# Layer 1's attention of a two-layer decoder trunk: the heads' first keys move from its prologue into the first step's filler

## What is computed

```python
h = x @ w_in_b[j]                                   # layer 1: 768 + 768 + 768 + 256 columns
q, k, v, q_mem = jnp.split(h, [qb, 2 * qb, 2 * qb + vb], axis=-1)
o = diff_attention(q, k, v, lam, slopes_b)          # softmax of two halves of a head, a = p0 - lam * p1
mix = rms_norm(o, subln_g[j]) * (1.0 - lam_init)
mem_out = memory_attention(q_mem, mem, w_mem_kv[i])
y = jnp.concatenate([mix, mem_out], axis=-1) @ w_out[i]
x = layer_norm(DN_ALPHA * x + y, ln_g[i, 0], ln_b[i, 0])
f = moe_ffn(x, ...)                                 # 64 experts, top 8 of 4 groups, one shared expert
x = layer_norm(DN_ALPHA * x + f, ln_g[i, 1], ln_b[i, 1])
```

## Time and profile before

| | |
|---|---|
| median of three runs | 1210.28 us (1208.69 to 1210.51) |
| profiled execution, its time | 1209.24 us |
| its span | 1207.3 us, granted clock 0.997 |
| TensorE busy | 1158.9 us (96%) |
| VectorE, ScalarE, GpSimd busy | 346.2, 299.5, 64.0 us |
| moved by DMA | 446.92 MB, 370 GB/s in the mean |

### The profile page before, as it was taken

The page is one execution under the profiler, slowest core; times in us unless marked ns, Lnnn a source line. Parts: engine busy times, 40 slices in busy tenths (PEclk is TensorE's granted clock), DMA queues, the critical chain, the costliest instruction groups (busy, mean ns, idle before and its releaser), DMA issues.

```text
span 1207.3 us, 22685 instructions
## 1 busy us (share of the span) xinstructions
PE 1158.9 (96%) x8946; PEld 708.4 (59%) x8948; DVE 346.2 (29%) x904; ACT 299.5 (25%) x713; POOL 64.0 (5%) x102
## 2 busy tenths in 40 slices
PE   9999999999999999998999999999999899999985
PEld 6875755555555555555687648555555555555552
DVE  1435612222122212221514456221222222222214
ACT  1453312222121212221213433122221212122212
POOL 1341000000001000000012100000000010000000
PEclk9999999999999999999999999999999999999998
DMA  9943799999999999999990558999999999999995
GB/s 359 365 176 128 308 414 416 421 422 422 422 422 420 410 420 421 422 421 420 389 361 24 203 233 335 410 419 421 422 422 422 422 415 403 404 421 422 422 421 209
DMA packets 74502, 446.92 MB, mean 370 GB/s; under 512 B 6976, under 2 KB 12480, under 8 KB 24896
## 3 DMA queue, kind: packets, MB, share of 16 engines
q1 hardware_dynamic: 72208, 441.22, 89.4%
q10 hardware_dynamic: 2224, 4.72, 1.0%
HBM read 444.86 MB, written 1.05 MB: 369 GB/s over the span
## 4 chain that ended last, share of the span: by engine, by line
PE 74%; DMA 17%; issue 4%; DVE 2%; POOL 1%; SPq 0%; ACT 0%; DVEq 0%; POOLq 0%
DMA ring<-in_w_up 16%; PE bank L1235 16%; PE bank L1216 14%; PE bank L1269 14%; PE bank L772 7%; PE bank L791 6%; PE bank L1277 4%; PE bank L830 4%; PE bank L1242 1%; PE bank L1092 1%; PE bank L806 1%; PE bank L1115 1%; PE bank L993 1%; POOL soft L731 1%; PE bank L761 1%
## 5 line engine op out<-in xcount | busy, mean ns | idle before, releaser
L1235 PE MATMUL bank<-ring,work 128*64 128x256 f32 x1952 | 225.4, 380 | 13.2 <-DMA ring<-in_w_up 13.0
L1216 PE MATMUL bank<-ring,work 128*64 128x256 f32 x1984 | 227.8, 382 | 8.9 <-DMA ring<-in_w_gate 8.7
L1269 PE MATMUL bank<-ring,work 128*32 128x512 f32 x1904 | 222.0, 595 | 0.3
L1216 PEld LDWEIGHTS bank<-ring,work 128*64 128x64 f32 x1984 | 141.3, 137 | 116.9 <-issue 58.1
L1235 PEld LDWEIGHTS bank<-ring,work 128*64 128x64 f32 x1952 | 147.5, 137 | 81.5 <-issue 20.4
L1938 DVE SCALAR_TENSOR_TENSOR yhalf<-bank,gcol,yhalf 128x512 fp32r<-128x512 f32 x124 | 93.1, 751 | 214.7 <-ACT yhalf L1562 214.7
L1930 DVE TENSOR_TENSOR work<-work,bank 128x256 f32<-128x256 f32 x64 | 26.9, 421 | 366.7 <-PE bank L1235 366.7
L1562 ACT ACTIVATE yhalf<-bank,gcol 128x512 fp32r<-128x512 f32 x124 | 85.2, 687 | 181.4 <-PE bank L1269 181.4
L1269 PEld LDWEIGHTS bank<-ring,work 128*32 128x32 f32 x1904 | 57.4, 109 | 116.9 <-issue 110.0
L1399 ACT ACTIVATE work<-bank 128x512 f32<-128x512 f32 (+4 forms) x177 | 77.9, 440 | 98.0 <-PE bank L772 46.3
L1399 ACT ACTIVATE back<-bank 128x128 fp32r<-128x128 bf16 x64 | 17.7, 277 | 280.5 <-PE bank L1188 280.5
(11 more groups left out here) (190 smaller groups left out, 819.1 us busy)
## 6 DMA issues: line engine op xcount, KB each, us to landing
ring<-in_w_gate SPq DMA_DIRECT2D x124, 1024.0 KB, 13.7
ring<-in_w_up SPq DMA_DIRECT2D x122, 1024.0 KB, 15.7
ring<-in_w_down SPq DMA_DIRECT2D x119, 1024.0 KB, 14.9
ring<-in_w_in_b SPq DMA_DIRECT2D x3, 3072.0 KB, 18.6
ring<-in_w_out SPq DMA_DIRECT2D x4, 2048.0 KB, 14.6
home<-in_w_gate SPq DMA_DIRECT2D x4, 1024.0 KB, 17.9
ring<-in_w_down SPq DMA_DIRECT2D x8, 512.0 KB, 13.3
ring<-in_w_in_a ACTq DMA_DIRECT2D x1, 3072.0 KB, 19.5
```

Of the source, the lines that this page charges most:

```text
L1216: last = pe.matmul(gate_bank[slots_of(e), 0:HID], xg[:, k, slots_of(2 * j + e)], w[e][:, k, :], start=(k == 0), stop=(k == KT - 1))
L1235: last = pe.matmul(up_bank[slots_of(e), 0:HID], xg[:, k, slots_of(2 * j + e)], w[e][:, k, :], start=(k == 0), stop=(k == KT - 1))
L1269: last = pe.matmul(yb[half][rows_of(t, e), :], hT[b][:, f, slots_of(e, t)], w[e][:, f, half * 512:half * 512 + 512], start=(f == 0), stop= ...
```

## The change

It takes k0 (and the wait for its weight item in1) out of the prologue of layer 1 and puts it into filler 0. q0 moves from filler 0 to filler 1, k1 from 1 to 2, where it stands before va; vb moves from filler 2 to 3, before q1. The table of groups gets k0 behind qm. The copies out of the banks move with their groups: VectorE's of k0, k1 and vb, ScalarE's of q0. From filler 4 on all is as it was, and banks, slots and the order of the loads are untouched.

```diff
-        [("km", "D", (0,)), ("x", "DADA", (2, 3, 4, 5)), ("vm", "A", (1,)), ("k0", "D", (0,)), ("qm", "A", (2,)),
+        [("km", "D", (0,)), ("x", "DADA", (2, 3, 4, 5)), ("vm", "A", (1,)), ("qm", "A", (2,)), ("k0", "D", (0,)),
...
                     for n in range(4):
                         evacuated(pe, G[1, "x"] + n)
-                    landed(pe, (1, "in1"))
                     wk, wq = item_view((1, "in1"), 768), item_view((1, "in0"), 768)
-                    tiles("k0", wk, 0, xT, 0, 16)
                     landed(pe, (1, "in3"))
                     tiles("qm", item_view((1, "in3"), 256), 0, xT, 0, 16)
...
                     if d == 0:
+                        landed(pe, (1, "in1"))
+                        tiles("k0", wk, 0, xT, 0, 16)
+                    elif d == 1:
                         landed(pe, (1, "in0"))
                         tiles("q0", wq, 0, xT, 0, 16)
-                    elif d == 1:
+                    elif d == 2:
                         tiles("k1", wk, 256, xT, 0, 16)
-                    elif d == 2:
                         landed(pe, (1, "in2"))
                         token_values("va", 0, 0)
+                    elif d == 3:
                         token_values("vb", 1, 0)
-                    elif d == 3:
                         tiles("q1", wq, 256, xT, 0, 16)
...
-                        if d in (0, 3):
+                        if d in (1, 3):
                             n = d // 3
                             take(scaled, qT[:, 2 * n:2 * n + 2, :], f"q{n}", 2, SEQ)
...
-                    take(copy, kT[:, 0:2, :], "k0", 2, SEQ)
...
-                        if d == 1:
+                        if d == 0:
+                            take(copy, kT[:, 0:2, :], "k0", 2, SEQ)
+                        elif d == 2:
                             take(copy, kT[:, 2:4, :], "k1", 2, SEQ)
...
-                        elif d == 2:
+                        elif d == 3:
                             take(copy, v[:, 1:2, 0:384], "vb", 1, 384)
```

## The result

The changed kernel takes 1218.65 us in the median of four runs (1217.47 to 1219.05); the kernel before takes 1210.39 us in four (1208.69 to 1211.86). The ratio is 1.0068, with a 95% interval from 1.0056 to 1.0079: slower by 0.7%. The profiled execution has a time of 1218.73 us and a span of 1216.6 us, 9.3 us above the span before.

The account below looks back on a forecast made before the run. The prediction took TensorE's own work to bound the attention stage, not the weight stream. It added 7.0 us for k0's cover, 1.7 for the clock and 0 for fillers and copies: +8.7 on 1210.28, giving 1219.0 us, range 1215.3 to 1221.7.

Parts of the forecast that it names:

- The cover: Layer 1 prologue: without k0 ahead of qm, in3's landing is no longer covered, and later steps come 7.0 us later.
- The fillers and the copies: Steps 1 to 3: longer fillers gain 0 (at most 1.7 us), moved copies cost 0 (at most 1 us).
- The idle time: Ahead of qm: TensorE idle 6.8 us, from vm's end at 604.9 until in3 lands and qm starts at 611.67.
- The clock: At qm: TensorE's clock falls to 1.2 GHz in the idle time, costing 1.7 us, bounds 0 to 3.4.
- The row that gave the 1.7: Kernel start: first eight warm-up matmuls took 3.55 us, against 1.9 at the later rate, so a slow start cost 1.7 us.
- The sum: On TensorE's path: 7.0 for the cover, 1.7 for the clock, 0 for fillers and copies, +8.7 us.
- the 627.4 that the prediction names: A sign in the changed kernel: batch 0's scores near 627.4, two and a half microseconds or less from the old 625.7.
- A: Rival at the wait ahead of qm: the clock holds, only 7.0 us are lost, time 1217.3; chance 0.20.
- D: Rival at qm: the clock's return takes twice as long, 7.0 plus 3.4 us, time 1220.7; chance 0.12.
- B: Rival in the expert stage: expert loads absorb the delay, so not slower, 1208 to 1210; chance 0.03.
- C: Rival at qm: in3 already in place at 604.9, so k0's move is a plain exchange, 1210.3; chance 0.03.

Follow-up runs that it names:

- the two halves of the change: Kernel before with only q0, k1 and vb moved later, k0 kept in the prologue: 1.0006; kernel before with only k0 moved to filler 0: 1.0072.
- the early in3: Changed kernel with in3 put into the resident gate matrices' buffer and issued right behind in1, gate matrices loaded after qm: 1210.90 us, ratio 1.0003.
- 8 dummies: Changed kernel with 8 warm-up matmuls of zeros, read by nobody, ahead of the wait for in3: 1218.77 us, ratio 1.0064.
- the second set of runs: The changed kernel, unaltered, taken once more beside the kernel before: 1219.98 us, ratio 1.0073 (1.0056 to 1.0090).
- 20 dummies: Changed kernel with 20 warm-up matmuls of zeros, read by nobody, ahead of the wait for in3: 1217.09 us, ratio 1.0053.
- q0 first: Kernel before with q0 and k0 exchanged, q0 ahead of qm in the prologue and k0 in filler 0: 1216.62 us, ratio 1.0040.

## Why the prediction was right

*Where the time is lost.* It named the wait of qm for in3 and the fall of the clock in it, and put every other part of the change at nothing; the two halves of the change (1.0006 and 1.0072) and the early in3 (1.0003) show it. What made this readable from the trace of before was one entry of 0.29 us in the weight loads: a wait that is nearly nothing because a tile of 7 us stands in front of it.

*The cover, 7.0 us.* Right. Steps 1 to 3 of the changed kernel end 9.4 us late, where batch 0's scores were 2.5 us late (628.18 against 625.69), so the moved tile itself is 6.9 us; with the clock held the last matmul comes 7.2 us late.

*The fillers and the copies, 0.* Right within what the halves can tell. VectorE's copy of k0 ran from 628.36 to 629.05 and was over before the first score copy, at 629.39; that one comes 2.4 us later than before, as do the scores.

*The idle time, 6.8 us.* It is 5.72. Before the edit is reached TensorE is already 0.6 us later than in the profile of before (vm ends at 605.5, not 604.9), and in3 lands within 5.4 us of its issue, not 6.7. qm starts at 611.16 by its first weight load, 0.5 us before its old start. By the prediction's own words it is wrong if in3 lands earlier than 6 us after its issue, and it did: this part of it failed. It held the landing time fixed, though its row was one draw, and it had a reading of the queue wrong. It took the 0.42 share in 605 to 607 to mean that no long backlog stood ahead of in3. But in0, 3072 KB, issued at 587.52 in the kernel before, landed 21.4 us later, at 608.9, which is 4.0 us after in3's issue. The first line is SyncE's timeline, the second the DMA view, both of the kernel before:

```profile
587.52 1.36 SPq L414 DMA_DIRECT2D ring<-in_w_in_b  x1
...
ring<-in_w_in_b SPq DMA_DIRECT2D x1, 3072.0 KB, 21.4
```

No run separates how much of in3's landing time is owed to in0's tail. In the eight profiles in which qm waited for in3, its first weight load came 5.4 to 6.8 us behind the issue, with TensorE at work meanwhile or idle.

*The clock, +1.7 us.* The mechanism was right, the size was one draw too: 17.06 - 14.0 = 3.1 us in the profiled execution, 15.74 - 14.0 = 1.7 in the second profile of the same kernel, 1.8 with only k0 late, 1.7 with 8 dummies. The bounds of 0 to 3.4 hold all of them. What differs is how much of the low level lies over work: from 611.2 to about 617.3 in the first, from 612.5 to about 615.9 in the second. The row that gave the 1.7 is a weak source: at the kernel's start the granted clock reads 1.00 from 1.3 to 4.7 us, so that its slow matmuls are slow by the clock is read from their length alone. That two later profiles came to the same 1.7 us is in part luck.

*The sum.* So the prediction's sum of 8.7 came to 9.35 in this pair of profiles (the last matmul is at 1203.97, against 1194.62): -0.5 for qm's earlier start, +3.1 for the clock and +6.9 for the tile, 9.5 less 0.1 of reading error. In the medians of the result it is 8.3 us (6.8 to 9.6 by the interval), the forecast 8.7. Part of that closeness is luck: in the profile the wait was 1.1 us shorter than the 6.8 forecast and the clock 1.4 us dearer, and the two errors nearly cancel. (The 9.35 holds, besides, the 0.6 us by which TensorE was late before the edit.) For the same reason batch 0's scores came at 628.18, near the 627.4 that the prediction names, and not by its route: qm took some 10 us (an estimate from 6.1 us at the low level and the rest at full rate) in place of 8.7.

*The rules of the skill.* The Trainium skill, "TensorE: Matmul & The Clock Gate", section "HAM oscillation — how this bites in real kernels", has a DMA wait of a few microseconds throttle the array, at a cost of half the throttled time. This case's traces agree: 0.50 behind the wait, and a cost of 3.1 us for 6.1 us of work at that level. The Trainium skill, "DMA: Bandwidth & Descriptors", section "Anatomy of one DMA — SWDGE (gpsimd) path", has a fit that gives an estimate of 4.4 us for 1 MB. It was made for GpSimd's path, while SyncE issues in3, and it stays below all landings of in3 measured here in its old place, which were 5.3 to 6.7 us.

*The rivals.* A (the clock holds) fell by the clock's rows; its time alone, 7.0 us above, lies inside the interval of the loss. It held where the idle time was 1.2 and 2.15 us. D (the clock at twice its price) is close to what the profiled execution of the changed kernel shows, 3.1 of 3.4 us, and the next one does not show it; its loss of 10.4 us lies above the interval of the result, which ends at 9.6, but inside that of the second set of runs (up to a ratio of 1.0090). B (absorbed by the expert stream) fell: TensorE's waits for expert weights are 12.6 and 8.7 us, as before, and DMA is at rest from 649 to 687 as it was from 640 to 678. C (in3 is not the last thing) fell with in3's landing at 610.9, just ahead of qm, and with the loss that went when in3 was early.

```profile
PE bank L1235 <- DMA ring<-in_w_up: 12.6, 12, 1.5
PE bank L1216 <- DMA ring<-in_w_gate: 8.7, 8, 1.1
PE bank L791 <- DMA ring<-in_w_in_b: 5.7, 1, 5.7
```

```profile
649.00:687.00 38.00, 38.00 (x194) 27.31 (x193) 12.95 (x51) 12.36 (x49) 4.57 (x6) 1.00 0.00 1
```

## What to carry to other kernels

A wait of 0.3 us in a trace may be the last tip of a wait of 6 us. Before a tile is moved, ask of each wait behind it when its semaphore is raised, not how long it lasts now: here the issue of in3 and its landing gave a wait of 6.8 us, and 5.7 us were measured. The clock's fall comes on top, and its price is not fixed: 1.7 and 3.1 us in two profiles of one kernel. And work that is moved out of such a place should leave as much behind as the transfer takes, or the transfer should be given a buffer that lets it start earlier; only then can the order of the tiles be chosen freely.

## What the runs showed of the hardware

The granted clock fell 5.0 us after the last matmul in one profile of the changed kernel and 2.2 us after it in another of the same kernel. It fell 3.0 us after it with only k0 late, 2.3 us with q0 first, and 4.4 us at the end of the kernel before. In the run with 20 dummies it fell 3.7 us after the last of them, when real matmuls had been running for 1.3 us. Waits of 1.2 and 2.15 us left it alone in one profile each. A wait of 2.4 us behind 20 dummies thus cost 1.8 us more than its own length, and did so after it was over.

A drop of the DMA share is not the landing of the transfer in front: with q0 first the share was 0.43 to 0.50 from 605 to 607 us, and in0 landed at 609.3 and was in use from 609.5.
